# The conditioning projection of a decoder step: from one block ahead of everything to eight units, six of them between the steps of attention

## The chip, the cores and the metric

The kernel runs on one core of one Trainium2 chip. The metric is the time of one execution in device microseconds, from the first to the last instruction of the core. Three runs of the kernel before took 3728.18, 3729.02 and 3730.79 us.

## The reference, cut to what matters

One step of a two-layer decoder trunk for a prompt of 512 tokens and 8 sample sequences, D_MODEL 1024, all in float32. Each sub-layer is steered by a conditioning vector c: a linear map gives its shift, scale and gate. Layer 0 mixes tokens by latent attention, layer 1 by pooling; both are followed by a mixer that gathers 128 experts for each token.

```
def adaln(c, w, b):
    return jnp.split(jax.nn.silu(c) @ w + b, 6, axis=-1)      # w: (1024, 6144) for each of two layers

for l in range(DEPTH):
    sp = adaln(c_prompt, w_ada[l], b_ada[l])                  # 1 row
    ss = adaln(c_sample, w_ada[l], b_ada[l])                  # 8 rows
    hp = modulate(rmsnorm(xp, norm_mix[l]), sp[0], sp[1])     # then the mixer: attention or pooling
    xp = xp + sp[2][:, None, :] * mp
    hp = modulate(rmsnorm(xp, norm_ffn[l]), sp[3], sp[4])
    xp = xp + sp[5][:, None, :] * peer(hp, w_peer_q[l], peer_subkeys[l], peer_u[l], peer_v[l])
```

So the projection multiplies 9 rows by two matrices of 1024 x 6144: 50.3 MB of weights. Of its 2 x 6 parts of 1024 columns, the first three of layer 0 are wanted by the first normalization; the next two by the experts' first normalization, at the end of attention; the rest later.

## The kernel before

The program writes out each engine's instructions in order, and semaphores join them. Nothing reorders it: what stands first on an engine or on SP's DMA queue goes first. It has three stages.

**Projection.** 24 blocks of 512 columns (12 a layer). SP loads a block of 2 MB into one of four slots of the big buffer; TensorE multiplies it by `cact`, silu of c, 128 x 9 for each of 8 row chunks, into bank 0 or 1 (8 matmuls of 512 columns; in float32 the profile shows two instructions for each); VectorE adds the bias into a stage; SP stores the 9 x 512 result to `ada_rows` in DRAM. Behind block 18, SP reads the first parts of layer 0 back (`mods`, `sample_mods`). The attention weights are loaded behind the last blocks, since they lie in the same buffer.

**Attention of layer 0.** Five token tiles: the samples (8 rows) first, then four prompt tiles of 128. The steps on TensorE are `latents` (transposes of h, then 16 matmuls by w_in, in two halves), `project` (transposes of z, 9 matmuls by w_uq, 4 by w_uk), `turn_heads` (24 transposes), `sample_absorb`, and for each prompt tile `attend` and `mix_out`. ScalarE copies each result out of its bank, VectorE normalizes (`latents_norm`, `rows_norm`, `heads_norm`). The order up to the first `attend`: latents 0, latents 1, project 0, project 1, latents 2, turn_heads 1, project 2, sample_absorb, latents 3. This is the stretch that the change fills. `w_out`, the output projection's weights, is loaded into the ring behind it.

**Experts.** A loop of turns t from -25. From turn 0 on each turn handles two experts of every token of a tile: GpSimd gathers their rows of 1 MB each into 8 slots by indirect DMAs, VectorE forms dots, ScalarE the activation, TensorE accumulates (L1056). The work beside it is tied to turn numbers: queries and key scores of the eight heads (L908, L923), for which SP loads `wk`, one load a head, two buffers; and the cached pages of the sample sequences, which SP loads through a page table, and which TensorE first turns at turn 1. Before turn -25, SP has loaded `wk` of heads 0 and 1; then it waits for `x_mixed` (the last add of attention), loads the page table, four rows of modulation and 16 pages, and only then enters the turns, in which the load of head 2 stands first. TensorE multiplies by it from turn -2 on (`queries`), between the two matmul groups of L967 that spread the first tile's hidden rows for VectorE (L1829).

Of the kernel before, what the change touches and what calls it, by code (L numbers as in the profile page):

```python
# [50 lines left out]
ADA = 6 * D  # L51

# [30 lines left out]
def decoder_step(nc, T, O):  # L83

    ctx = ExitStack()
    with ctx:
# [49 lines left out]
        w_ada = big[:, :].rearrange("p (s c n) -> p s c n", s=4, c=DC)  # L136
# [22 lines left out]
        qs_s = ring[:, 0:2, :].rearrange("p a n -> p (a n)")[:, 0:NH * QH]  # L159
        ks_s = ring[:, 2, :]  # L160
# [16 lines left out]
        cact = hbuf[:, 2, 0:DC * NC].rearrange("p (c n) -> p c n", c=DC)  # L177

        ada_stage = work[0:NC, W - D:W].rearrange("p (b n) -> p b n", b=2)

        def ada_bias(l):
            return work[0:NC, 0:ADA] if l == 0 else ring[0:NC, 0:6, :].rearrange("p a n -> p (a n)")
# [92 lines left out]
        LAST_OUT = -14  # L275
        rows_of = lambda n: P if n < S0 else SROWS
# [86 lines left out]
        for name in ("first_in", "first_set", "own_used", "o_ready0", "o_ready1", "x_in", "consts_in", "c_in", "b_in", "table_in", "mix_w_in0", "mix_w_in1", "mix_w_in2", "mix_w_in3", "mix_w_in4", "out_w_in", "gains_in", "rot_in",  # L363
                     "mods_in", "pool_in", "state_in", "rows_out", "own_out", "own_in",
                     "y_out", "state_out", "dve_step", "act_step", "slot_turn", "gain_s_in", "pool_gain_in", "smp_mods_in", "link_done", "wait_done", "rank_step", "smp_step", "gate_in", "smp_gate_in", "wk_in0", "wk_in1", "pst_out", "mix_w_free", "smp_w_in0", "smp_w_in1"):
            sem(name)
# [4 lines left out]
        def _(sp):  # L371
# [7 lines left out]
            for l in range(DEPTH):  # L379
                ld(ada_bias(l),  # L380
                   T["b_ada"][l].partition_broadcast(NC), "b_in")
# [12 lines left out]
            def store_ada(i):  # L394
                l, j = divmod(i, ADA // 512)
                ld(ada_rows[l, :, j * 512:(j + 1) * 512], ada_stage[:, i % 2, :], f"ada_out{i % 2}")

            for l in range(DEPTH):
                for j in range(ADA // 512):
                    i = l * (ADA // 512) + j  # L400
                    if i >= 4:
                        sp.wait_ge(sem("ada_ps"), i - 3)
                    ld(w_ada[:, i % 4], T["w_ada"][l].rearrange("(c p) n -> p c n", p=P)[:, :, j * 512:(j + 1) * 512],
                       f"ada_w_in{i % 4}")
                    if i == 3:
                        for t in range(NT):
                            ld(x_tok[:, t, :], T["x_prompt"][0, t * P:(t + 1) * P, :], "x_in")
                        ld(x_tok[0:NS, NT, :], T["x_sample"].rearrange("b s d -> (b s) d"), "x_in")
                    if i >= 2:
                        sp.wait_ge(sem("ada_row"), i - 1)  # L410
                        store_ada(i - 2)
                    if i == ADA // 512 + 6:

                        for k in range(2):
                            sp.wait_ge(sem(f"ada_out{k}"), 16 * (ADA // 512 // 2))
                        mods(mod_mix, 0, 0, "prompt", P, T["norm_mix"][0])
                        sample_mods(0, 0)

            blocks = 2 * ADA // 512
            for n_, (dst, src, size) in enumerate(((w_in, T["w_mla_in"][0], DC * ZW), (w_uq, T["w_uq"][0], QLC * NH * QH),  # L420
                                                   (w_uk, T["w_uk"][0].rearrange("c h d -> c (h d)"), KLC * NH * NOPE),
# [1474 lines left out]
```

## Time and profile before

| | |
|---|---|
| Runs, median (lowest to highest) | 3729.02 us (3728.18 to 3730.79) |
| Profiled execution: time, span | 3729.29 us, 3727.5 us |
| TensorE busy | 2980.5 us (80%) |
| VectorE, ScalarE, GpSimd busy | 2313.5, 1049.1, 1221.7 us |
| Moved by DMA | 1266.81 MB, mean 340 GB/s |
| Chain that ended last | PE 45%, DMA 25%, DVE 15%, issue 7%, ACT 4% |

PE is TensorE, PEld its weight loads, DVE VectorE, ACT ScalarE, POOL GpSimd, SP the engine that issues most DMAs. A row of the timeline gives the start, how long the merged instructions lasted, engine, line, operation, tiles and count, and in brackets how long the engine had been idle and what ended that. The span has three parts: the projection until about 187 us, attention until about 628 us, and the expert turns, which fill the rest and move most of the bytes.

### The profile page before, as it was taken

How to read it: one execution, taken by the hardware profiler on the slowest of the kernel's cores; microseconds unless marked ns; L12 is line 12 of the kernel's file. 1: busy time of each engine (PE TensorE's matmuls, PEld its weight loads, DVE VectorE, ACT ScalarE, POOL GpSimd, SP SyncE). 2: the span in 40 equal slices, each digit the busy share in tenths (PEclk: the TensorE clock that was granted, in tenths of full speed). 3: DMA queues.
4: the chain of work that ended last, by engine and by line, in shares of the span. 5: the costliest groups of instructions: out<-in, count | busy, mean ns of one | idle time of the engine just before them, and what ended most of it. 6: DMA issues, size and time to landing. Idle time of an engine off the chain costs nothing.

```text
span 3727.5 us, 39795 instructions
## 1 busy us (share of the span) xinstructions
PE 2980.5 (80%) x11339; PEld 1299.6 (35%) x11339; DVE 2313.5 (62%) x6432; ACT 1049.1 (28%) x4465; POOL 1221.7 (33%) x1061
## 2 busy tenths in 40 slices
PE   8977886797888985898989868979876775586757
PEld 1235554443434432343444334434321231122311
DVE  0155444688778785677777576777866545555463
ACT  0012221343343441343444413434311111111111
POOL 0000000243333332443444434434444344434452
PEclk9987898898999997899999989999987777667775
DMA  9911002799999998999999999999999999979996
GB/s 316 333 52 60 33 1 109 300 402 360 415 359 383 413 402 323 403 413 400 411 413 392 418 360 416 404 404 412 392 409 405 422 415 410 347 266 413 421 420 168
DMA packets 217305, 1266.81 MB, mean 340 GB/s; under 512 B 22867, under 2 KB 43620, under 8 KB 77283
## 3 DMA queue, kind: packets, MB, share of 16 engines
q0 software_dynamic: 150016, 1090.59, 72.9%
q1 hardware_dynamic: 67069, 173.69, 12.6%
q8 instruction: 90, 1.47, 0.2%
q14 instruction: 130, 1.06, 0.1%
HBM read 1260.86 MB, written 3.79 MB: 339 GB/s over the span
## 4 chain that ended last, share of the span: by engine, by line
PE 45%; DMA 25%; DVE 15%; issue 7%; ACT 4%; POOL 2%; SPq 2%; DVEq 0%; POOLq 0%; ACTq 0%; PEldq 0%
PE bank L1056 16%; DMA ring<-in_uv,work 11%; PE bank L796 7%; DMA mod_mix<-in_uv,work 7%; DMA big<-in_uv,work 5%; PE bank L908 5%; PE bank L600 4%; DVE ring L1842 2%; PE bank L813 2%; PE bank L739 1%; PE bank L626 1%; ACT work L1330 1%; PE bank L651 1%; SPq L375 1%; POOL ring L1363 1%
## 5 line engine op out<-in xcount | busy, mean ns | idle before, releaser
L1056 PE MATMUL bank<-ring,work 128*64 128x512 f32 (+1 forms) x2112 | 945.2, 720 | 269.9 <-ACT work L1330 269.6
L1363 POOL DMA_INDIRECT ring<-in_uv,work x528 | 614.8, 1164 | 968.5 <-PE bank L1056 868.5
L1842 DVE CUSTOM_DVE_ANT_0 ring<-ring,mod_smp 128x1024 f32<-128x1024 f32 x512 | 621.9, 1224 | 261.9 <-DMA ring<-in_uv,work 253.1
L1363 POOL DMA_INDIRECT big<-in_uv,work x264 | 314.0, 1189 | 1088.5 <-DVE work L1733 623.8
L1317 ACT ACTIVATE work<-work 128x2 f32<-128x2 f32 (+1 forms) x528 | 107.3, 203 | 1542.6 <-DVE work L1842 1538.3
L796 PE MATMUL bank<-big 128*128 128x512 f32 x1024 | 516.6, 628 | 0.0
L1056 PE MATMUL bank<-big,work 128*64 128x512 f32 (+1 forms) x1056 | 332.6, 734 | 154.9 <-ACT work L1330 153.8
L1056 PEld LDWEIGHTS bank<-ring,work 128*64 128x64 f32 (+1 forms) x2112 | 215.4, 153 | 657.6 <-ACT work L1330 387.4
L1842 DVE CUSTOM_DVE_ANT_0 big<-big,mod_smp 128x1024 f32<-128x1024 f32 x256 | 309.8, 1224 | 141.6 <-DMA big<-in_uv,work 136.1
L1056 PE MATMUL bank<-work 128*64 128x512 f32 (+1 forms) x528 | 306.6, 709 | 105.3 <-ACT work L1330 104.8
L1330 ACT ACTIVATE work<-small,work 128x64 f32<-128x64 f32 (+1 forms) x1056 | 309.3, 340 | 192.9 <-DVE work L1853 136.4
L1182 ACT ACTIVATE bank<-bank 128x128 f32<-128x128 f32 x1024 | 270.1, 264 | 171.4 <-PE bank L796 155.0
L1056 PE MATMUL bank<-mod_mix,work 128*64 128x512 f32 (+1 forms) x528 | 317.7, 732 | 0.0
L908 PE MATMUL bank<-big 128*128 128x256 f32 x1024 | 237.3, 386 | 40.3 <-DMA big<-in_wk 39.0
L1363 POOL DMA_INDIRECT work<-in_uv,work x132 | 145.8, 1105 | 373.5 <-PE bank L1056 363.9
L796 PEld LDWEIGHTS bank<-big 128*128 128x128 f32 x1024 | 176.1, 192 | 215.4 <-issue 212.1
L908 PEld LDWEIGHTS bank<-big 128*128 128x128 f32 x1024 | 194.7, 193 | 89.1 <-DMA big<-in_wk 40.7
L1853 DVE TENSOR_TENSOR work<-work 128x2 f32<-128x2 f32 (+1 forms) x528 | 82.1, 155 | 219.3 <-ACT work L1317 210.2
L1842 DVE CUSTOM_DVE_ANT_0 mod_mix<-mod_mix,mod_smp 128x1024 f32<-128x1024 f32 x128 | 156.6, 1223 | 93.2 <-DMA mod_mix<-in_uv,work 93.2
L1056 PEld LDWEIGHTS bank<-big,work 128*64 128x64 f32 (+1 forms) x1056 | 76.3, 154 | 357.1 <-ACT work L1330 178.4
L1182 ACT ACTIVATION_READ_ACCUMULATOR bank<-bank 128x1 f32 x1024 | 193.6, 189 | 0.0
L1842 DVE CUSTOM_DVE_ANT_0 work<-work,mod_smp 128x1024 f32<-128x1024 f32 x128 | 156.6, 1224 | 43.5 <-DMA work<-in_uv,work 40.9
(277 smaller groups left out, 3634.0 us busy)
## 6 DMA issues: line engine op xcount, KB each, us to landing
big<-in_wk SPq DMA_DIRECT2D x48, 1152.0 KB
big<-in_w_ada SPq DMA_DIRECT2D x24, 2048.0 KB, 8.6
work<-in_cache_mla SPq DMA_DIRECT2D x104, 160.0 KB
ring<-in_uv,work POOLq DMA_INDIRECT x528
big<-in_uv,work POOLq DMA_INDIRECT x264
ring<-in_w_mla_out SPq DMA_DIRECT2D x1, 4096.0 KB, 13.3
big<-ada_rows SPq DMA_DIRECT2D x8, 512.0 KB, 7.4
big<-in_w_mla_out SPq DMA_DIRECT2D x4, 1024.0 KB, 13.1
```

The costliest lines, as they stand in the source:

```text
L375: sp.dma_start(dst, src).then_inc(sem(name), 16)
L600: last = mm(pb[i % 2][0:NC, :], cact[:, c, :], w_ada[:, i % 4, c, :], start=(c == 0), stop=(c == DC - 1))
L796: last = mm(pb[2 + half][:, :], cachedT[:, c * P:(c + 1) * P], w_uk[:, c, half * 512:(half + 1) * 512], start=(c == 0), stop=(c == KLC - 1))
L813: last = mm(pb[6][0:NH, 160:160 + KL], ps_s[:, g, :], cached[g][:, 0:KL] if g < NPG else cached_own, start=(g == 0), stop=(g == NPG))
L908: last = mm(pb[0][:, side * 2 * P:(side + 1) * 2 * P], wk[i % 2][:, c * 2 * NK + side * NK:c * 2 * NK + (side + 1) * NK], hT2[:, c, :], st ...
L1056: last = mm(out, diag[0:rows, t % 2, j, 0:min(m, HALF)], s[0:rows, D + half * 512:D + (half + 1) * 512], start=(k == 0 and (n < S0 or j == ...
L1182: last = act.activation(k, k, ACT.Square, accum_out=kss[:, at:at + 1])
L1317: act.activation(acts[0:m, t % 2 * GRP:(t % 2 + 1) * GRP], dots[0:m, t % 2 * GRP:(t % 2 + 1) * GRP], ACT.Gelu)\
L1330: act.activation(diag[0:m, t % 2, j, 0:o], scale_rows, ACT.Copy, scale=wts[0:m, at:at + 1]).then_inc(sem("diag_set"), 1)
L1363: pool.indirect_dma_start(slot[g % SLOTS][0:m, :], None, T["uv"].rearrange("l e d -> (l e) d"), bass.IndirectOffsetOnAxis(index[0:m, k * G ...
L1842: dve.tensor_tensor_reduce(u, u, hb[0:m, :], 1.0, 0.0, ALU.mult, ALU.add, dots[0:m, at:at + 1]).then_inc(sem("dots_set"), 1)
L1853: tt(wts[0:m, cols], acts[0:m, cols], g_all[0:m, k * GRP:(k + 1) * GRP], ALU.mult).then_inc(sem("wts_set"), 1)
```

## The change

The projection is cut into 8 units of 1536 columns (4 a layer). A unit has 9 slices: 8 of 128 rows of weights (128 x 1536, 786 KB) and one that is the bias row, multiplied by a row of ones. A slice is 4 matmuls of 384 columns; each writes another group of 32 partitions of one bank, so each uses another 32 columns of the array. `cact` is padded with zeros from 9 to 32 columns. Four slots in the ring hold slices. Units 0 and 1 come first; the 54 slices of the other six are put into the steps up to the first `attend` by `ADA_PLAN`, 0 to 4 at each of 19 points. ScalarE copies a finished unit out of its bank (in place of VectorE's bias adds), GpSimd stores it in four DMAs (in place of SP's stores). To free banks 6 and 7, early transposes go to banks 4 and 5, with waits for `z_ready`. Attention weights have their place from the start, so w_in and w_uq are loaded beside the units. SP's block that waits for `x_mixed`, with page table and pages, moves behind the loads of heads 2 and 3, to turn -5.

```
+UNIT = ADA // 4
+UGRP = UNIT // 4
+NSLICE = DC + 1
+ADA_SLOTS = 4
+        ada_bank = lambda u: pb[u if u < 2 else 7]
+        ADA_PLAN = (0, 2, 2, 2, 3, 3, 3, 3, 3, 3, 3, 3, 3, 3, 3, 3, 4, 4, 4)
# SP
+            def ada_slices(a, b):
+                for n in range(a, b):
+                    u, c = divmod(n, NSLICE)
+                    l, k = divmod(u, 4)
+                    if n >= ADA_SLOTS:
+                        sp.wait_ge(sem("ada_used"), n - ADA_SLOTS + 1)
+                    cols = slice(k * UNIT, (k + 1) * UNIT)
+                    if c < DC:
+                        ld(ada_slot[n % ADA_SLOTS], T["w_ada"][l, c * P:(c + 1) * P, cols], f"ada_w_in{n % ADA_SLOTS}")
+                    else:
+                        ld(ada_slot[n % ADA_SLOTS][0:1, :], T["b_ada"][l:l + 1, cols], f"ada_w_in{n % ADA_SLOTS}")
+            ada_slices(0, ADA_SLOTS)
+            ld(x_tok[0:NS, NT, :], T["x_sample"].rearrange("b s d -> (b s) d"), "x_in")
+            for t in range(NT):
+                ld(x_tok[:, t, :], T["x_prompt"][0, t * P:(t + 1) * P, :], "x_in")
+            ada_slices(ADA_SLOTS, NSLICE + 5)
+            load_mix_w(0)
+            ada_slices(NSLICE + 5, 2 * NSLICE)
+            load_mix_w(1)
+            ada_stored(2)
+            mods(mod_mix, 0, 0, "prompt", P, T["norm_mix"][0])
+            sample_mods(0, 0)
...
+            ada_slices(2 * NSLICE, 2 * NSLICE + ADA_SLOTS)
...
+            ada_slices(2 * NSLICE + ADA_SLOTS, UNITS * NSLICE)
             for i, t in enumerate(mla_order):
                 w.next("row_ready")
...
+                    sp.wait_ge(sem("ada_used"), UNITS * NSLICE)
+                    ada_stored(UNITS)
                     ld(w_out, T["w_mla_out"][0].rearrange("(c p) n -> p c n", p=P), "out_w_in")
...
+                if t == -5:
+                    sp.wait_ge(sem("x_mixed"), NT)
+                    ld(pages, T["page_table"].rearrange("(a s) g -> a (s g)", a=1), "table_in")
...
+                    load_pages(0)
# TensorE
+            def ada_slices(count):
+                for _ in range(count):
...
+                    pe.wait_ge(sem(f"ada_w_in{n % ADA_SLOTS}"), 16 * (n // ADA_SLOTS + 1))
+                    if c == 0 and u >= 3:
+                        pe.wait_ge(sem("ada_row"), u)
+                    k = slice(0, P) if c < DC else slice(0, 1)
+                    for g in range(4):
+                        last = mm(ada_bank(u)[g * UROWS:(g + 1) * UROWS, 0:UGRP], cact[:, c, :] if c < DC else ones[0:1, 0:UROWS],
+                                  ada_slot[n % ADA_SLOTS][k, g * UGRP:(g + 1) * UGRP], start=(c == 0), stop=(c == DC))
+                    last.then_inc(sem("ada_used"), 1)
# project(i) on TensorE
+                zq, zk = (pb[4], pb[5]) if i <= 2 else (pb[6], pb[7])
+                if i <= 2:
+                    pe.wait_ge(sem("z_ready"), (2, 2, 3)[i])
# ScalarE
+                act.activation(ada_stage[u % 2], ada_bank(u)[:, 0:UGRP], ACT.Copy).then_inc(sem("ada_row"), 1)
# GpSimd
+                for g in range(4):
+                    at = k * UNIT + g * UGRP
+                    pool.dma_start(ada_rows[l, :, at:at + UGRP], ada_stage[u % 2][g * UROWS:g * UROWS + NC, :]).then_inc(sem(f"ada_out{u % 2}"), 16)
```

On TensorE at the start of the program, before: L600 is the projection, L609 transposes of h, L626 the matmuls of `latents`, L640 to L643 the transposes of `project`, L651 and L654 its matmuls.

```order
L600 MATMUL bank<-big,hbuf 9x512 x192
L609 MATMUL bank<-small,hbuf 128x8 x8
L626 MATMUL bank<-big,hT 8x352 x16
L609 MATMUL bank<-small,hbuf 128x128 x8
L626 MATMUL bank<-big,hT 128x352 x16
L640 MATMUL bank<-small,hbuf 128x8 x3
```

The same place of the program now (line numbers have moved: L609 is the projection, L628 and L650 are transposes and matmuls of `latents`, L667 the first transposes of `project`):

```order
L609 MATMUL bank<-ring,work 32x384 x32
L609 MATMUL bank<-ring,ones 32x384 x4
L609 MATMUL bank<-ring,work 32x384 x32
L609 MATMUL bank<-ring,ones 32x384 x4
L628 MATMUL bank<-small,hbuf 128x8 x8
L650 MATMUL bank<-big,hT 8x352 x8
L609 MATMUL bank<-ring,work 32x384 x8
L650 MATMUL bank<-big,hT 8x352 x8
L628 MATMUL bank<-small,hbuf 128x128 x8
L609 MATMUL bank<-ring,work 32x384 x8
L650 MATMUL bank<-big,hT 128x352 x8
L609 MATMUL bank<-ring,work 32x384 x8
```

Of 192 matmuls of 512 columns, 72 of 384 columns are left in front; the others stand between the steps.

On SP's queue at the end of attention, before (`out_rows_p` are stores of latent rows, `in_wk` the heads' weights):

```order
L375 DMA big<-ada_rows 128x1024 x2
L375 DMA out_rows_p<-work 128x320 x2
L375 DMA big<-in_norm_ffn 128x1024
L375 DMA big<-in_wk 128x2304 x2
L375 DMA big<-in_page_table 1x128
L375 DMA work<-ada_rows 128x1024 x3
L375 DMA work<-in_norm_ffn 128x1024
```

The same place now:

```order
L380 DMA big<-ada_rows 128x1024 x2
L380 DMA out_rows_p<-work 128x320 x2
L380 DMA big<-in_norm_ffn 128x1024
L380 DMA big<-in_wk 128x2304 x4
L380 DMA big<-in_page_table 1x128
L380 DMA work<-ada_rows 128x1024 x3
L380 DMA work<-in_norm_ffn 128x1024
```

Two more loads of `in_wk` stand ahead of the page table; before, they stood behind the 16 page loads.

## Rows read from the trace of the kernel before

**Rows 1.** Chain that ended last, 0 to 700: start, us, what.
```profile
2.58 13.90 DMA big<-in_w_ada
16.62 118.67 PE bank L600 x272
...
186.59 1.24 DVE mod_mix L1399
```
**Rows 2.** Windows: length, busy us of each engine, TensorE clock, DMA share, GB/s.
```profile
40.00:60.00 20.00, 20.00 (x47) 4.18 (x46) 1.52 (x3) 0.00 (x0) 0.00 (x0) 1.00 1.05 384
50.00:100.00 50.00, 50.00 (x118) 10.63 (x117) 4.75 (x7) 0.00 (x0) 0.00 (x0) 1.00 0.92 321
```
**Rows 3.** DMA issues 0 to 620: KB each, median us to landing.
```profile
ring<-in_w_mla_out SPq DMA_DIRECT2D x1, 4096.0 KB, 13.3
```
**Rows 4.** Timeline of GpSimd and SP: issues of a gather, of a store.
```profile
626.18 0.94 POOL L1363 DMA_INDIRECT big<-in_uv,work  x1 [0.31 <-issue]
129.21 0.28 SPq L375 DMA_DIRECT2D ada_rows<-work  x1
```
**Rows 5.** Timeline of SP: rows read back, and the issue behind them.
```profile
136.47 1.31 SPq L375 DMA_DIRECT2D mod_mix<-ada_rows  x3
139.52 0.40 SPq L375 DMA_DIRECT2D big<-in_w_ada  x1
```
**Rows 6.** Timeline of TensorE, expert turns: two 64-column groups, and what follows.
```profile
700.32 0.64 PE L1056 MATMUL bank<-ring,work 128*64 128x512 f32 x1
700.33 0.64 PE L1056 MATMUL bank<-mod_mix,work 128*64 128x512 f32 x1
700.80 0.59 PE L1056 MATMUL bank<-ring,work 128*64 128x512 f32 x1
705.15 1.94 PE L1056 MATMUL bank<-big,work 128*64 128x512 f32 x8
707.02 1.98 PE L796 MATMUL bank<-big 128*128 128x512 f32 x4
```
**Rows 7.** Timeline of TensorE's weight loads there.
```profile
700.80 0.14 PEld L1056 LDWEIGHTS bank<-ring,work 128*64 128x64 f32 x1 [0.29 <-issue]
```
**Rows 8.** What TensorE waited for, 194 to 330: total, times, longest.
```profile
PE bank L626 <- ACT hT L1078: 6.8, 4, 3.7
PE bank L663 <- DVE hbuf L1483: 4.4, 1, 4.4
PE bank L640 <- issue: 3.9, 1, 3.9
PE bank L651 <- ACT work L1078: 3.8, 3, 1.4
PE bank L675 <- ACT hbuf L1078: 3.4, 1, 3.4
PE bank L640 <- ACT ring L1078: 3.3, 1, 3.3
```
**Rows 9.** Timeline of ScalarE: z copied out; TensorE: last step before `attend`, first of `mix_out`.
```profile
223.11 0.96 ACT L1078 ACTIVATE hbuf<-bank 128x352 f32<-128x352 f32 x2 [11.30 <-PE bank L626]
314.72 12.62 PE L626 MATMUL bank<-big,hT 128*128 128x352 f32 x32 [1.37 <-ACT hT L1078]
358.77 3.60 PE L739 MATMUL bank<-ring,hbuf 128*128 128x512 f32 x8
```
**Rows 10.** Timeline, end of attention: TensorE, VectorE, SP.
```profile
624.16 3.55 PE L967 MATMUL bank<-hbuf,small 128*64 128x512 f32 x8
666.72 6.38 PE L908 MATMUL bank<-big 128*128 128x256 f32 x16 [39.01 <-DMA big<-in_wk]
675.02 1.29 DVE L1829 TENSOR_SCALAR mod_smp<-bank 128x512 f32<-128x512 f32 x2 [39.67 <-PE bank L967]
634.69 20.05 SPq L375 DMA_DIRECT2D work<-in_cache_mla  x13
```
**Rows 11.** Windows there, columns as in rows 2.
```profile
625.00:670.00 45.00, 5.99 (x16) 3.11 (x13) 9.18 (x38) 2.37 (x3) 7.45 (x8) 0.54 0.92 354
670.00:685.00 15.00, 11.93 (x53) 7.36 (x51) 8.96 (x26) 3.05 (x8) 1.44 (x2) 0.93 0.04 9
```

More of the change, by code:

```diff
@@ L158, in decoder_step @@
         z_s = hbuf[:, 2, 0:ZW]
-        qs_s = ring[:, 0:2, :].rearrange("p a n -> p (a n)")[:, 0:NH * QH]
-        ks_s = ring[:, 2, :]
+        ring_all = ring[:, :, :].rearrange("p a n -> p (a n)")
+        ada_slot = [ring_all[:, j * UNIT:(j + 1) * UNIT] for j in range(ADA_SLOTS)]
+        qs_s = ring_all[:, ADA_SLOTS * UNIT:ADA_SLOTS * UNIT + NH * QH]
+        ks_s = hbuf[:, 2, :]
+        ada_stage = [pT[0][:, 0:UGRP], ring_all[:, ADA_SLOTS * UNIT + NH * QH:ADA_SLOTS * UNIT + NH * QH + UGRP]]
+        ada_bank = lambda u: pb[u if u < 2 else 7]
         rot_at = ZW + QH + NOPE + NH * QH
@@ new lines, in ada_stored, with load_mix_w @@
+            def ada_stored(units):
+                for k in range(2):
+                    sp.wait_ge(sem(f"ada_out{k}"), 16 * 4 * units // 2)
+            mix_w = ((w_in, T["w_mla_in"][0]), (w_uq, T["w_uq"][0]), (w_uk, T["w_uk"][0].rearrange("c h d -> c (h d)")),
+                     (w_uv, T["w_uv"][0].rearrange("c h d -> c (h d)")))
+            def load_mix_w(k):
+                ld(mix_w[k][0], mix_w[k][1].rearrange("(c p) n -> p c n", p=P), f"mix_w_in{k}")
+            ada_slices(0, ADA_SLOTS)
@@ L467, in _ @@
             sp.wait_ge(sem("first_set"), 1)
-            sp.wait_ge(sem("x_mixed"), NT)
-            ld(pages, T["page_table"].rearrange("(a s) g -> a (s g)", a=1), "table_in")
-            mods(mod_ffn, 0, 3, "prompt", P, T["norm_ffn"][0], gain)
-            sp.wait_ge(sem("rows_out"), 16 * (NT + 1))
-            sp.wait_ge(sem("own_out"), 16)
-            ld(s_own, own_dram.rearrange("(a s) h -> a (s h)", a=1), "own_in")
-            w.next("smp_clear")
-            w.next("table_in", 16)
             def load_pages(r):
@@ L594, in _, with ada_point @@
             w.next("c_act")
-            for i in range(2 * ADA // 512):
-                w.next(f"ada_w_in{i % 4}", 16)
-                if i >= 2:
-                    pe.wait_ge(sem("ada_row"), i - 1)
-                for c in range(DC):
-                    last = mm(pb[i % 2][0:NC, :], cact[:, c, :], w_ada[:, i % 4, c, :], start=(c == 0), stop=(c == DC - 1))
-                last.then_inc(sem("ada_ps"), 1)
+            w.next("ones_set")
+            ada_at = [0]
+            def ada_slices(count):
+                for _ in range(count):
+                    n = ada_at[0]
+                    ada_at[0] += 1
+                    u, c = divmod(n, NSLICE)
+                    pe.wait_ge(sem(f"ada_w_in{n % ADA_SLOTS}"), 16 * (n // ADA_SLOTS + 1))
[6 more added lines that the diff above has]
+                    last.then_inc(sem("ada_used"), 1)
+            ada_point_no = [0]
+            def ada_point():
+                if ada_point_no[0] < len(ADA_PLAN):
+                    ada_slices(ADA_PLAN[ada_point_no[0]])
+                ada_point_no[0] += 1
+            ada_slices(2 * NSLICE)
             def transpose_h(t, hb):
@@ L624, in latents @@
                 for half in range(2):
+                    if half:
+                        ada_point()
                     for c in range(DC):
@@ L762, in _ @@
                     latents(t + 4)
-            w.next("ones_set")
             def turn_page(r, g):
```

136 lines of the change are left out of this document (68 added, 68 removed).

## The prediction

> **What bounds the kernel now.** I read the chain that ended last first. Until 187 us it is the projection alone: a load until 16.6 us, then L600 on TensorE, and VectorE's first use of the modulation at 186.59 [rows 1]. The windows say why: TensorE is busy for the whole of each, at full clock, with 2.36 matmul instructions a microsecond, each 512 columns in 0.43 us [rows 2]. The DMA engines carry 321 to 384 GB/s beside it, so TensorE ends last, DMA close behind. Only 9 of the array's 128 columns are in use. Second, the waits of TensorE between 194 and 330 us: the six long ones sum to 25.6 us [rows 8], none of them for a DMA. The DMA queue has little to do there: the w_out load is nearly the only big one. Third, the timeline where attention ends: TensorE stands for 39.01 us before the queries of head 2, until `wk` lands, and VectorE 39.67 us behind it for L967; SP spends that time on pages [rows 10]. From 670 to 685 us the DMA engines carry 9 GB/s [rows 11].
>
> **Part 1, the projection in front.** It loses 6 of its 8 units. What is left is either bound by bytes or by columns.
> Bytes: slice 17 is landed behind 16 slices of 0.786 MB (12.6), the tokens (2.1) and w_in (2.9): 17.6 MB. At 384 GB/s [rows 2] that is 46 us; it starts at 2.58 us [rows 1] and lands some 2.8 us after its last byte (w_out, 4.19 MB in 13.3 us [rows 3], is 10.9 us of data and 2.4 more): 51 us. Before reads its weights in rows of 2 KB, the change in rows of 6 KB; I leave the rate.
> Columns: the nearest row is L1056, where two groups of 64 columns are in use. Both groups' instructions start together (700.32 and 700.33) and the next pair starts 0.48 us later; eight instructions and the switch to a full-array matmul take 1.87 us (705.15 to 707.02) [rows 6], where serial ones would take 3.4. Their weight loads of 0.14 us lie inside [rows 7]. So two groups overlap fully. Four groups of 384 columns, two instructions each, are 8 x 0.32 = 2.57 us in series and 0.64 us if four overlap as two do. The bounds are these two; I take 0.64, since the row that shows column groups shows them in parallel, and 0.15 us for a switch of groups (1.87 less 4 x 0.43). 18 slices are then 12 us, far under the loads' pace of 2.05 us a slice: DMA bound. In series they would be 46 us, still level with it.
> Behind slice 17: 1.3 us of TensorE, 0.5 us of ScalarE's copy, then GpSimd's four stores. The trace has no plain store from GpSimd; its gathers take 0.94 us and 0.30 us between them, SP's stores 0.28 us [rows 4]. I take the gathers' 1.25 us: 5.0 us, and 2.4 us to land. SP then issues the reads back, 3.05 us until the next issue [rows 5], of 2.2 MB (5.8 us) plus 2.4 us to land, say 8.5 us. Sum: 51 + 1.3 + 0.5 + 5.0 + 2.4 + 8.5 = 69 us, against 186.6: **118 us earlier**. Ends: stores at SP's 0.28 us and loads at 400 GB/s give 62; loads at 321 GB/s [rows 2] give 78: 108 to 125.
>
> On DMA the Trainium skill (DMA: Bandwidth & Descriptors, Specifications) gives about 358 GB/s as the HBM limit for a core; by it the 17.6 MB would take 49 us and the forecast be 3 us later. The trace disagrees: 384 here [rows 2].
>
> **Part 2, six units inside attention.** 54 slices at 0.64 us plus a switch for each of 18 bursts are 37 us of TensorE. I walked the steps in order, adding each burst, and took it out where TensorE waits anyway: bursts behind transposes (ScalarE copies 1.4 us meanwhile), behind project 0, 1 and 2 (3.3 to 3.7 us), and before turn_heads 1 and project 2 (4.4 and 3.9 us) [rows 8]. That hides about 19 of the 37; of the 25.6 us of waits not all lie where a burst stands. 18 us stay on the path, mostly the bursts between matmul groups.
> The refill: a burst of three needs one slice already there and two whose slots came free in the burst before. At 2.05 us of data and 2.4 to land they are there 6.5 to 7 us later. Steps of 8 to 10 us (w_uq's matmuls, a half of `latents`) cover that, and the 3.45 us of w_uk's is followed by a wait. Only the last bursts, of four slices with short steps between, come too close: in my walk 4 us of waiting before latents 3's matmuls, and 1 us in `sample_absorb`, where slice 63 needs bank 7, which ScalarE empties only after the q_abs copies.
> New wait for banks 4 and 5: project 0's transposes now wait until ScalarE has copied z, 0.96 us [rows 9], on the path: 1.2 us. Project 1's and 2's are long satisfied. In the queue: the gains are issued behind 3.1 MB of attention weights and four slices, 17 us of data; they are wanted some 23 us behind the modulation, so they fit, just. Behind 50 slices SP stands until TensorE has used slice 67; row stores and `own_scores` are late, and nobody waits for them until the pages. w_out is issued 7 us after slice 71 (copy, stores) and takes 13.3 us [rows 3]; latents 3's second half and `attend` lie between slice 71 and `mix_out`, and from 327 to 358.77 us `attend` alone is 31 us [rows 9]. Hidden. The bias adds that VectorE loses were off the path.
> Two to three microseconds more for slices that meet the clock at 1.2 GHz. **Together 26 us later**: 18 + 5 + 1.2 + 2. Ends: with the bursts wholly in the waits, and less of the stretch at half clock, 10; with nothing hidden (37) and twice the refill waits, 50.
>
> **Part 3, head 2 ahead of the pages.** Its load now waits only for head 0's scores and lands some 20 us before TensorE wants it. The L908 at 666.72 can follow the L967 that ends at 627.7, so TensorE and VectorE's L1829 could come 39 us earlier [rows 10]. What is late next is DMA: the first gathers, modulation and pages. Between 625 and 670 us 354 GB/s x 45 = 15.9 MB moved [rows 11]; heads 2 and 3 (1.18 MB each) leave that traffic for an idle stretch. 14.7 MB at 384 to 400 are 37 to 38 us, so DMA is through at 663 and goes on with the next gathers, which before began at 683-685; with head 3's 3 us that is 25. So 25 us if the turns that follow are DMA bound, 39 if they aren't. Page issues begin when they did (the table waits for `x_mixed`), 13 in 20.05 us [rows 10], and turn 1 needs only four. I take 30 us earlier. Lowest end 10 us, if turn 1 waits for its pages behind eight gathers.
>
> **Sum.** The profiled execution took 3729.29 us, 0.3 above the median of the runs: 3729 - 118 + 26 - 30 = **3607 us**. Everything behind hangs on turn order and keeps its length.
>
> **Rivals.**
> *The groups don't overlap* (2.57 us a slice). For it: four groups are nowhere in the trace. Against: two overlap fully. 54 slices are 139 us more less 25.6 of cover, 113; the front some 3 more; 3729 - 115 + 113 + 1 + 2 - 30 = 3700. 6%.
> *Weight loads stay exposed.* Four groups bring 8 weight loads a slice; at 0.14 us each [rows 7] outside the matmuls a slice is 1.8 us: 54 x 1.12 = 60 us more, 8 of it hidden: 3659. Against: L1056's lie inside. 5%. The Trainium skill has the rule behind this (TensorE: Matmul & The Clock Gate, Part 3): weight loads overlap running matmuls only if they address other row groups, and here all groups use all rows. By it this rival would be the forecast; rows 6 and 7 show the contrary for two groups that share all rows.
> *The ring of four is too small*: a slice lands 8 us after its slot is free, and each of 17 bursts waits 2 to 3 us: 3645. For it: only two or three loads are in flight. Against: the pace of [rows 2]. 8%.
> *The 39 us come back*: the first turns wait for pages or gathers, and part 3 gives 5: 3632. 8%.
> *Slower than before*: groups in series and at half clock, since the bursts keep being interrupted: 5.1 us a slice, 277 us in attention less 25 of cover, 92 instead of 49 us in front: 3729 - 118 + 43 + 252 + 3 - 30 = 3879. It decides from the slice cost at which 54 of them, less the cover, eat 118 + 30, about 3.2 us a slice. 2%.
>
> **How the numbers follow.** The forecast has 71%; its own range, 118 (-10, +7), 26 (-16, +24) and 30 (-20, +9), not all at their ends together, is 3583 to 3642. The range for 8 in 10 takes in the two near rivals and part of the weight loads': 3580 to 3652. 0.2% (7.5 us) is about what a measurement can tell from no change. Only the serial rival at half clock is slower; cases between it and no gain get 1% each way: faster 0.96, same 0.01, slower 0.03.
>
> **What would show it.** The first modulation product on VectorE near 69 us, not 187, with DMA at 380 GB/s before it and TensorE mostly waiting for slices. A slice's eight instructions in 0.64 to 0.7 us; 2.57 would mean series, 1.8 exposed loads. In the stretch from there to the first `attend`, 141 us before, some 166 now, with waits for slices of a few us in total and none for w_out. At the end of attention no wait for `wk`, and L1829 right behind the second L967. I am wrong if TensorE's waits for slices sum to over 15 us, if the reads back land after 80 us, or if the distance from the last `mix_out` to the first expert turn shrinks by less than 20 us.

## The result, and the profile after

The changed kernel takes 3600.55 us (median of 4 runs, 3592.32 to 3605.52) where the kernel before took 3728.6 us beside it: a ratio of 0.9652, with a 95% interval of 0.9636 to 0.9669. The forecast was 3607 us with a range of 3580 to 3652. The profiled execution is the fastest of the four, 3592.32 us with a span of 3590.5.

**The front.** The timeline of VectorE shows its first modulation product, which was at 186.59 [rows 1], and the chain that ended last shows the way to it (start, us, what):

```profile
68.76 1.23 DVE L1463 SCALAR_TENSOR_TENSOR mod_mix<-mod_mix,hT 128x1024 f32<-128x1024 f32 x1 [62.98 <-DMA hT<-in_norm_mix]
```
```profile
37.50 14.04 DMA ring<-in_w_ada
51.58 2.98 PE bank L609 x16
54.59 0.50 ACT ring L1124
55.13 0.53 issue
55.66 1.53 POOL ada_rows L1413 x3
57.19 1.69 DMA ada_rows<-ring
...
60.28 8.35 DMA hT<-in_norm_mix
```

The last slice of weights is used at 51.58, where the working had it landed at 51. Behind it come a slice and a bias slice on TensorE, ScalarE's copy of the bank, GpSimd's stores and the reads back. TensorE now waits for slices for 28.7 us of the front, which the groups by line say (0 to 68 us; busy us, mean ns of one, idle before):

```profile
L609 PE MATMUL bank<-ring,work 128*32 128x384 f32 x128 | 23.5, 825 | 28.7 <-DMA ring<-in_w_ada 28.7
```

and the windows (columns as in [rows 2]) show the DMA engines full instead of TensorE, which is busy for 25.78 of 48 us; its slices take 1.51 us each there, at half clock:

```profile
7.00:55.00 48.00, 25.78 (x144) 3.62 (x144) 0.00 (x0) 0.90 (x2) 2.22 (x4) 0.75 1.01 393
55.00:69.00 14.00, 0.00 (x0) 0.00 (x0) 0.24 (x1) 0.08 (x1) 2.04 (x4) 0.50 0.68 201
```

**Attention.** Latents 0 starts at 77.2 us and `attend(0)` at 230.8; before it was 194.9 and 327.2 (the window below begins at 194.8). That stretch has grown from 132.4 to 153.6 us. Here it is in one window, first of the kernel before, then of the changed one:

```profile
194.80:327.20 132.40, 105.00 (x329) 56.27 (x330) 68.36 (x185) 22.62 (x46) 0.00 (x0) 0.82 0.14 51
```
```profile
77.20:230.80 153.60, 137.66 (x761) 59.81 (x762) 68.20 (x184) 25.52 (x52) 12.29 (x24) 0.92 0.69 252
```

TensorE was idle for 27.4 us of it, and now for 15.9. Its groups by line there give the bursts 48.0 us (weight slices and bias slices):

```profile
L609 PE MATMUL bank<-ring,work 128*32 128x384 f32 x384 | 41.9, 530 | 7.9 <-DMA ring<-in_w_ada 7.1 <-ACT work L1124 0.8
L609 PE MATMUL bank<-ring,ones 1*32 1x384 f32 x48 | 6.1, 582 | 0.0
```

All other matmuls of the stretch, the same work as before, took 137.7 - 48.0 = 89.7 us instead of 105.0. The granted clock goes with it: 0.92 instead of 0.82. So the 21.2 us are 48.0 for bursts, less 15.3 us that the other matmuls took less at the higher clock, less 11.5 us of idle time. The timeline of TensorE shows slices at full clock (8 instructions in 0.85 us alone, 24 in 2.14, so 0.65 for each further slice and 0.71 on average) and a place where it goes wrong:

```profile
138.32 2.14 PE L609 MATMUL bank<-ring,work 128*32 128x384 f32 x24
140.39 3.70 PE L683 MATMUL bank<-big,work 128*128 128x512 f32 x8
...
147.49 0.85 PE L609 MATMUL bank<-ring,work 128*32 128x384 f32 x8
150.55 1.29 PE L609 MATMUL bank<-ring,work 128*32 128x384 f32 x8 [2.20 <-DMA ring<-in_w_ada]
151.77 1.50 PE L609 MATMUL bank<-ring,ones 1*32 1x384 f32 x8
153.20 7.19 PE L650 MATMUL bank<-big,hT 128*128 128x352 f32 x16
160.32 2.14 PE L609 MATMUL bank<-ring,work 128*32 128x384 f32 x24
162.39 5.00 PE L650 MATMUL bank<-big,hT 128*128 128x352 f32 x16
```

The wait of 2.20 us is for a slice of the ring, and behind it sixteen matmuls take 7.19 us, where the same number takes 5.00 a little later. A second such place is at 211.81: waits of 2.48, 0.94 and 0.43 us for slices, and 5.90 us for the sixteen matmuls. In a third TensorE is at work throughout: the 32 matmuls of 8 columns in `sample_absorb`, 196.7 to 202.0 us, have a granted clock of 0.68, and the two slices behind them take 2.79 us.

**The end of attention.** What stood in [rows 10] is answered by these of TensorE and VectorE: no wait for `wk`, and the pages' wait in its place.

```profile
535.53 3.72 PE L941 MATMUL bank<-big 128*128 128x256 f32 x16
...
537.55 1.28 DVE L1893 TENSOR_SCALAR mod_smp<-bank 128x512 f32<-128x512 f32 x2
...
563.82 0.69 PE L807 MATMUL bank<-small,work 128*128 128x128 f32 x2 [18.09 <-DMA work<-in_cache_mla]
```

Windows there, which answer to [rows 11]; no stretch at 9 GB/s is left:

```profile
527.50:572.50 45.00, 23.49 (x91) 12.43 (x89) 28.03 (x87) 10.36 (x29) 11.47 (x12) 0.71 0.99 374
572.50:587.50 15.00, 15.00 (x76) 6.76 (x72) 14.51 (x54) 7.28 (x40) 6.91 (x7) 1.00 0.98 402
```

The 25th gather on GpSimd is a good mark, since from there on both kernels do the same. Its row of before, and of after:

```profile
732.29 0.94 POOL L1363 DMA_INDIRECT big<-in_uv,work  x1 [2.45 <-PE bank L1056]
```
```profile
607.70 0.94 POOL L1433 DMA_INDIRECT big<-in_uv,work  x1 [2.47 <-PE bank L1089]
```

So up to this mark 124.6 us are gained: 117.8 in front (186.59 to 68.76), 21.4 given back from there to `attend(0)`, and 28.2 from `attend(0)` to the mark (405.1 us before, 376.9 now). From the mark to the end it is 2997.0 us before and 2992.9 by the median of the runs. In these two and the kernels below, which do the same there, the distance from the 25th to the 1045th gather lies between 2911 and 2924 us, so 4 us there mean nothing.

### The profile page after: what moved, and what is told of

It is laid out like the page before. It is cut to its first block, busy times and chain, and to the rows that moved or that the text cites. A ratio compares the mean times of both kernels' runs of the same rounds, so it can differ in the third digit from the quotient of the medians.

```text
span 3590.5 us, 40191 instructions
## 1 busy us (share of the span) xinstructions
PE 2848.8 (79%) x11531; PEld 1264.3 (35%) x11531; DVE 2295.5 (64%) x6409; ACT 1049.6 (29%) x4473; POOL 1224.3 (34%) x1093
## 3 DMA queue, kind: packets, MB, share of 16 engines
q8 instruction: 92, 1.51, 0.2%
## 4 chain that ended last, share of the span: by engine, by line
PE 42%; DMA 28%; DVE 15%; issue 7%; ACT 4%; POOL 2%; SPq 1%; DVEq 0%; POOLq 0%; ACTq 0%; PEldq 0%
PE bank L1089 17%; DMA ring<-in_uv,work 10%; DMA mod_mix<-in_uv,work 7%; DMA big<-in_uv,work 6%; PE bank L829 6%; PE bank L941 5%; DVE ring L1906 2%; DMA ring<-in_w_ada 2%; PE bank L846 2%; PE bank L650 2%; PE bank L774 2%; ACT work L1393 1%; DMA work<-in_cache_mla 1%; PE bank L609 1%; PE bank L679 1%
## 5 line engine op out<-in xcount | busy, mean ns | idle before, releaser
L1433 POOL DMA_INDIRECT ring<-in_uv,work x528 | 603.3, 1143 | 967.0 <-PE bank L1089 853.3
L829 PE MATMUL bank<-big 128*128 128x512 f32 x1024 | 509.4, 620 | 0.0
## 6 DMA issues: line engine op xcount, KB each, us to landing
ring<-in_uv,work POOLq DMA_INDIRECT x528, 11.5
big<-in_w_mla_out SPq DMA_DIRECT2D x4, 1024.0 KB, 11.5
```

Source lines behind the costliest of these rows:

```text
L829: last = mm(pb[2 + half][:, :], cachedT[:, c * P:(c + 1) * P], w_uk[:, c, half * 512:(half + 1) * 512], start=(c == 0), stop=(c == KLC - 1))
L1433: pool.indirect_dma_start(slot[g % SLOTS][0:m, :], None, T["uv"].rearrange("l e d -> (l e) d"), bass.IndirectOffsetOnAxis(index[0:m, k * G ...
```

## Experiments

All ratios are against the kernel before, timed on the same chip in the same session.

**1 and 2: part 3 undone, and part 3 alone.** In the changed kernel, the block with the page table, the FFN modulation and the pages goes back in front of the turns:

```diff
-                if t == -5:
+                if t == FIRST:
                     sp.wait_ge(sem("x_mixed"), NT)
```

> The changed kernel with SP's block (wait for x_mixed, page table, modulation, 16 pages) put back ahead of the loads of heads 2 and 3, nothing else undone. My theory: this part alone is worth the 27 us between the shift of the first gather (97.7 us earlier than before) and that of the gathers from the tenth on (about 125 us), so the time is 3628 us (3620 to 3636), with a wait of some 39 us for head 2's weights back in the trace. Rival: the order of the loads is worth nothing since DMA is saturated from there on anyway, and the 27 us come from the earlier start of something else: 3601 us.

Measured: 3621.49 us (3620.09 to 3627.27), ratio 0.9725 (0.9707 to 0.9743). Against 0.9652 that is 0.0073, or 27 us for part 3; the intervals of the two ratios make it 27 give or take 9. What TensorE waits for at the end of attention (500 to 600; total, times, longest) is again `wk`:

```profile
PE bank L941 <- DMA big<-in_wk: 38.3, 1, 38.3
```

In the kernel before, the same block moved behind the issue of `wk`, and nothing else:

```diff
             sp.wait_ge(sem("first_set"), 1)
-            sp.wait_ge(sem("x_mixed"), NT)
-            ld(pages, T["page_table"].rearrange("(a s) g -> a (s g)", a=1), "table_in")
...
-            load_pages(0)
...
+                if t == -5:
+                    sp.wait_ge(sem("x_mixed"), NT)
+                    ld(pages, T["page_table"].rearrange("(a s) g -> a (s g)", a=1), "table_in")
...
+                    load_pages(0)
```

> The kernel before with only that block moved to turn -5; the projection stays one block of 24 ahead of everything. Theory: the two parts of the change are independent and this one gives about 27 us: 3702 us (3693 to 3710). Rival: it pays only beside the new projection: 3729 us.

Measured: 3705.05 us (3703.72 to 3710.39), ratio 0.9947 (0.9928 to 0.9965), 20 us, give or take 7. TensorE's wait for `wk` is gone and this has come (600 to 700):

```profile
PE bank L775 <- DMA work<-in_cache_mla: 16.6, 1, 16.6
```

Its 25th gather is at 707.70, 24.6 us ahead of the kernel before. From `attend(0)` (329.27) to that gather it has 378.4 us against 405.1, which makes 26.7 us for part 3 beside the old projection; beside the new one it is 399.5 - 376.9 = 22.6 us, between experiment 1 and the changed kernel. These readings are sharper than the times, and the time of experiment 1 also has in it a stretch before `attend(0)` that is 6.9 us shorter (experiment 9). All of them lie at 20 to 27 us, not at the 39 of the wait that went. Of the 28.2 us gained between `attend(0)` and the mark, 5.6 stay when the block is put back (405.1 against 399.5); what gives them was not traced.

**3: is it the pages, or the bytes?** GpSimd holds its fifth gather, and with it those behind, until the first pages are in, so that pages and modulation don't share the DMA engines with them:

```diff
+                    if g == 4:
+                        pool.wait_ge(sem("page_in0"), 16 * PGRP)
+                        pool.sem_inc(sem("slot_turn"), 1)
```

> The changed kernel, but GpSimd issues the fifth to eighth gather only once the first four cached pages have landed. In the changed kernel TensorE stands 18.1 us at turn 1 for these pages, which share the DMA engines with eight gathers of 1 MB, while the DMA engines are busy throughout (share 1.0, 375 to 421 GB/s). Theory: the stretch is bound by bytes and the bytes are the same, so the wait shrinks to under 8 us and the time stays within 4 us of 3600. Rival: the wait is on the path, and the time falls by 8 to 15 us. Third: holding the gathers opens a hole in the DMA and costs up to 8 us.

Measured: 3598.36 us (3595.43 to 3605.64), ratio 0.9661 (0.9644 to 0.9677): no change. Yet the wait for pages (520 to 600) shrank from 18.1 us to this:

```profile
PE bank L807 <- DMA work<-in_cache_mla: 2.4, 1, 2.4
```

and the DMA engines are as full in the same windows as in the changed kernel:

```profile
527.50:572.50 45.00, 28.23 (x112) 13.74 (x110) 30.11 (x95) 12.06 (x39) 14.19 (x14) 0.83 0.98 377
572.50:587.50 15.00, 13.08 (x58) 5.70 (x55) 12.29 (x43) 5.17 (x31) 7.55 (x5) 1.00 1.01 421
```

The 25th gather came at 606.0 instead of 607.7. The order of the transfers decides who waits: VectorE now waits 15.8 us for gathers between 527 and 608 us, where it was 0.3. That fits a stretch bound by bytes, since the DMA engines have a share of 0.95 or more in both kernels up to that gather. It does not exclude TensorE: in the changed kernel it works without a gap from the pages' landing (563.82) to the 25th gather, which waits for it, and here from 582.92. So the wait for pages lies on the path. Shown is that it can't be traded for a wait for gathers at a profit, and not that it costs nothing.

**4: what the front's other loads cost.** The queue's order: 18 slices, then the tokens, the reads back, w_in, four slices, the gains, and only then the other attention weights.

```diff
-            ada_slices(0, ADA_SLOTS)
+            ada_slices(0, 2 * NSLICE)
...
-            ada_slices(ADA_SLOTS, NSLICE + 5)
-            load_mix_w(0)
-            ada_slices(NSLICE + 5, 2 * NSLICE)
-            load_mix_w(1)
...
-            load_mix_w(2)
-            load_mix_w(3)
-            ld(w_ukT, T["w_ukT"], "mix_w_in4")
+            load_mix_w(0)
...
+            for k in range(1, 4):
+                load_mix_w(k)
+            ld(w_ukT, T["w_ukT"], "mix_w_in4")
```

> The changed kernel with another order of loads in front: the 18 slices of units 0 and 1 first, then the tokens, then the modulation read back, then w_in and four slices, and the other attention weights behind the gains. Theory: the front is bound by bytes until slice 17 lands (17.6 MB, now 12.6 MB), so VectorE's first modulation product comes 12 us earlier than at 68.8 us and the time falls by 11 us, to 3589 (3583 to 3596). Rival: TensorE at 1.2 GHz (1.51 us a slice) or the ring of four slots sets the pace once no other loads stand between the slices, and less than 5 us are left: 3596 to 3601.

Measured: 3588.45 us (3584.24 to 3591.66), ratio 0.9629 (0.9613 to 0.9645). The first product is at 56.85, 11.9 us earlier, but `attend(0)` only 4.9 us (225.9), and the 25th gather 5.8 us (601.9). The median agrees with the expected 3589 us, but the trace shows only half of the 11 us behind it, and the interval overlaps that of the changed kernel; the hit is no proof of the theory. Here is what took most of the 7 us, in TensorE's timeline: slice 22 is late, and the matmuls behind the wait run at the lower clock.

```profile
92.91 1.51 PE L606 MATMUL bank<-ring,work 128*32 128x384 f32 x8 [5.10 <-DMA ring<-in_w_ada]
94.80 1.51 PE L606 MATMUL bank<-ring,work 128*32 128x384 f32 x8 [0.38 <-DMA ring<-in_w_ada]
96.24 7.29 PE L647 MATMUL bank<-big,hT 128*128 128x352 f32 x16
```

**5: without column groups.** Each chunk's four matmuls write the same 32 columns, summed, so that none can run beside another (ScalarE's copy and GpSimd's stores take these 32 partitions). The kernel leaves out three quarters of the modulation's columns.

```diff
-    last = mm(ada_bank(u)[g * UROWS:(g + 1) * UROWS, 0:UGRP], cact[:, c, :] if c < DC else ones[0:1, 0:UROWS],
-              ada_slot[n % ADA_SLOTS][k, g * UGRP:(g + 1) * UGRP], start=(c == 0), stop=(c == DC))
+    last = mm(ada_bank(u)[0:UROWS, 0:UGRP], cact[:, c, :] if c < DC else ones[0:1, 0:UROWS],
+              ada_slot[n % ADA_SLOTS][k, g * UGRP:(g + 1) * UGRP], start=(c == 0 and g == 0), stop=(c == DC and g == 3))
...
```

> The changed kernel, but the four matmuls of each chunk of a slice write the same 32 columns of the array (partitions 0 to 31 of the bank), one after the other, so no two of them can run side by side; ScalarE copies and GpSimd stores the same amount from there. It leaves out three quarters of the modulation's columns: each unit's four groups are summed into one. If column groups are what makes a slice cost 0.64 to 0.71 us, as the forecast has it, a slice is now 8 instructions of 384 columns in series, 2.57 us or a little more, 54 slices in attention cost some 103 us more, of which up to 6 lie in waits that are left, and the time is near 3697 us (3685 to 3715), with attend 0 some 97 us later than in the changed kernel. If the groups bring nothing and a slice is cheap for another reason (384 columns wide, 32 columns of weights), the time stays near 3600 us (3592 to 3612).

Measured: 3701.23 us (3700.17 to 3704.6), ratio 0.9924 (0.9908 to 0.994). 24 instructions, three slices, take 7.90 to 7.93 us in TensorE's timeline, against 2.14 above:

```profile
146.68 7.90 PE L609 MATMUL bank<-ring,work 128*32 128x384 f32 x24
154.41 3.60 PE L683 MATMUL bank<-big,work 128*8 128x512 f32 x8
```

That is 2.63 us a slice, close to the 2.57 of the forecast's rival of groups in series, which had 3700 us. The groups are worth 101 us: the stretch from latents 0 to `attend(0)` has 248.4 us, 94.8 more than in the changed kernel, and starts 8.9 us later. How four can overlap though every one needs its own weights shows in the weight loads of the changed kernel, then of this one (timeline of PEld):

```profile
144.02 0.16 PEld L609 LDWEIGHTS bank<-ring,work 128*32 128x32 f32 x8 [0.76 <-issue]
144.37 0.13 PEld L609 LDWEIGHTS bank<-ring,work 128*32 128x32 f32 x4 [0.19 <-issue]
```
```profile
147.00 0.11 PEld L609 LDWEIGHTS bank<-ring,work 128*32 128x32 f32 x1 [0.21 <-issue]
147.32 0.11 PEld L609 LDWEIGHTS bank<-ring,work 128*32 128x32 f32 x1 [0.21 <-issue]
```

With groups, four to eight loads lie within 0.13 to 0.16 us; without, one at a time, every 0.32 us. In neither kernel do they stand outside the matmuls: the series has 16 instructions in 5.35 us and 24 in 7.93, 0.32 for each.

**6: no bursts in attention.** All 72 slices in front, `ADA_PLAN = ()`.

> The changed kernel, but all 72 slices run in front of latents 0 and none inside attention; the column groups, the reads back of layer 0 after 36 slices, and the place of the pages' block stay. 64 weight slices of 0.786 MB, the tokens and w_in are 55.3 MB: at 390 GB/s TensorE is through with slice 71 near 148 us and latents 0 starts there, 71 us later than now (77). Against it stand the 21 us that bursts add to the stretch from the modulation to attend 0. Theory (bursts cost 21 us and hide DMA time of 71): 3600 + 71 - 21 = 3650 us (3642 to 3660). Rival (the bursts cost attention more than that stretch shows, up to the 47 us of their columns and waits): 3625 us or less. Rival (loads of attention's weights behind the slices then hold project 0): 3660 us or more.

Measured: 3672.65 us (3670.03 to 3686.74), ratio 0.9857 (0.9834 to 0.9879). The theory's time was missed by 23 us, and the wrong part was the front: latents 0 starts at 169.5 us, not 148. The second rival has the time (3660 or more) but not the cause: behind latents 0 TensorE waits for no load of weights. The expectation had left out the reads back and w_uq (4.6 MB, 12 us), and the rate fell:

```profile
55.00:148.00 93.00, 57.67 (x340) 8.23 (x344) 13.22 (x32) 2.46 (x5) 10.24 (x20) 0.60 0.96 364
```

From latents 0 to `attend(0)`, where the experiment speaks, it has 134.5 us without bursts, 19.1 less than the changed kernel and 2.1 more than before:

```profile
169.50:304.00 134.50, 106.98 (x332) 56.41 (x329) 62.84 (x169) 23.10 (x47) 2.05 (x4) 0.82 0.16 62
```

3600.5 + 92.3 - 19.1 = 3674, so the account closes. The row is also the control for the clock: new banks, waits and queue, but no bursts, and TensorE is at 0.82 and 107 us busy as in the kernel before. It is the bursts that bring 0.92. The other kernels agree: this stretch has 0.81 in experiment 2, without bursts, and 0.89 to 0.95 in each of those with them.

**7 and 8: other plans.** Experiment 7 is 4 with the plan (0,2,2,0,3,4,3,3,4,2,2,4,4,3,4,3,4,3,4); experiment 8 is the changed kernel with another plan alone.

```diff
-        ADA_PLAN = (0, 2, 2, 2, 3, 3, 3, 3, 3, 3, 3, 3, 3, 3, 3, 3, 4, 4, 4)
+        ADA_PLAN = (0, 2, 2, 2, 3, 4, 3, 3, 4, 2, 2, 3, 4, 3, 4, 3, 4, 2, 4)
```

> The changed kernel with the queue order of the experiment on the front (18 slices first, then the tokens, the reads back, w_in, four slices, the gains, the other attention weights, the remaining slices) and the plan (0,2,2,0,3,4,3,3,4,2,2,4,4,3,4,3,4,3,4): bursts are sized to the slices that can have landed by then. That order alone measured 3588 us with 10.5 us of waits for slices inside attention. If those waits are what gave back 7 of the 12 us that its front gained, they fall to 3 us or less and the time is 3582 us (3577 to 3587). If the time was given back by something else (the clock, the weights of project 0, the DMA behind), it stays at 3588 us (3585 to 3592).

> The changed kernel with its own queue order and another plan, (0,2,2,2,3,4,3,3,4,2,2,3,4,3,4,3,4,2,4): the same 54 slices, moved among the 19 places toward those behind which TensorE waits anyway. The changed kernel shows 7.1 us of waits for slices, and 2.2 us more of matmuls at the lower clock behind one of them. If these are what the place of the bursts decides, the time is 3594 us (3589 to 3598), with 3 us or less of waits for slices. If the total of slices that must be loaded between 58 and 215 us decides (260 GB/s of 400, so not bound), or the waits only move, it stays within 3 us of 3600.

Measured for 7: 3588.97 us (3581.56 to 3590.86), ratio 0.9614 (0.9599 to 0.9628), which is 3585 us beside a kernel before of 3728.6. The waits for slices did not fall (10.7 us against 10.5), but none is over 1.5 us, no group of matmuls behind one is slow, and `attend(0)` comes at 218.5, 7.4 us ahead of experiment 4. What TensorE waited for (55 to 330) in 7, then in 4 (55 to 230):

```profile
PE bank L606 <- DMA ring<-in_w_ada: 10.7, 12, 1.5
```
```profile
PE bank L606 <- DMA ring<-in_w_ada: 10.5, 7, 5.1
```

The time is the rival's (3588), not the theory's 3582. It is the fastest kernel measured: its interval is clear of the changed kernel's first one (0.9636 to 0.9669) and just touches the second (0.9626 to 0.9654, experiment 9). From experiment 4 it can't be told apart. Its theory named the wrong quantity, the sum of the waits, while the clock behind them is what moved: TensorE is busy for 135.9 us of the stretch instead of 141.4, at 0.94 instead of 0.89; 2.1 us more came from latents 0, which starts earlier. For 8: 3602.16 us (3599.55 to 3611.83), ratio 0.9667 (0.965 to 0.9685), no gain in the median. Its waits for slices total 7.2 us, as before, so the rival held: they moved. Its profile does reach `attend(0)` at 226.5 and the 25th gather at 603.2, 4.3 and 4.5 us earlier than the changed kernel's: gains of this size are lost in the 13 us by which the rest varies.

**9 and 10: once more, and a ring of three.** `ADA_SLOTS = 3` for the second.

> The changed kernel once more, in other executions, to see how much of the differences between the profiles of its attention stretch is the kernel's and how much the run's. Its first profile has 153.6 us from the start of latents 0 to attend 0, 7.1 us of them waits for slices, the longest 2.5 us, and matmuls of latents at the lower clock behind a wait of 2.2 us; the kernel that differs only far behind that stretch (pages' block early) had 146.7 us, 4.9 us of waits, the longest 1.2 us, and no such slow matmuls. Theory: the waits for slices vary from run to run and the clock follows the longer ones, so this stretch comes out anywhere between 146 and 155 us, with slow matmuls only behind a wait of about 2 us or more. Rival: the stretch is a fixed property of the kernel, and comes out at 153.6 within 1 us. Time 3600 us (3593 to 3607) in both.

> The changed kernel with three slots for slices in the ring instead of four. A burst of three then needs all three slots full, which takes some 2.4 us after the last matmul of the burst before plus 2.05 us for each slice still to come, up to 8.6 us, and each burst of four waits a further 4.5 us for its fourth slice. Theory (the ring's depth is what keeps the waits for slices at 7 us): they grow by 20 to 40 us, and the time is 3625 us (3612 to 3645). Rival (bytes per time decide, 260 GB/s of 400 over the stretch, and depth does not matter): waits of 12 us or less and 3605 us or less.

Measured for 9: 3598.84 us (3590.08 to 3601.31), ratio 0.964 (0.9626 to 0.9654). The stretch from latents 0 to `attend(0)` has 153.4 us, with the same two waits and the same slow matmuls:

```profile
150.26 1.47 PE L609 MATMUL bank<-ring,work 128*32 128x384 f32 x8 [2.33 <-DMA ring<-in_w_ada]
151.66 1.50 PE L609 MATMUL bank<-ring,ones 1*32 1x384 f32 x8
153.10 7.01 PE L650 MATMUL bank<-big,hT 128*128 128x352 f32 x16
```

The rival held: the stretch repeats within 0.2 us. Experiment 3 is a third profile of the same instructions up to there, taken on the chip and in the session of experiment 1, and has 153.5 us, with 7.29 us for the matmuls behind a wait of 2.21. Why experiment 1 had 146.7 us stays open: its slice landed about 1 us earlier and its clock stayed up. The chip and the session are excluded; whether it is the kernel or that one execution, a single profile can't say.

For 10: 3611.15 us (3605.72 to 3617.83), ratio 0.9672 (0.9658 to 0.9687), 12 us over experiment 9. The waits for slices doubled, the stretch took 165.0 us, 11.6 more, and it began 3.5 us later, since the front has the same ring:

```profile
PE bank L609 <- DMA ring<-in_w_ada: 14.5, 16, 2.3
```

Neither side had the size: the ring's depth matters, but the waits grew by 7 us where the theory asked for 20 to 40, and the time by half of the 25 it asked for. This kernel also shows that the length of a wait alone doesn't set the clock: behind its longest, the sixteen matmuls are not slow, while behind waits of 0.34 and 0.52 us (182.49, 184.38) the eighteen of w_uq take 10.80 us instead of 7.99.

```profile
159.26 0.85 PE L609 MATMUL bank<-ring,work 128*32 128x384 f32 x8 [2.30 <-DMA ring<-in_w_ada]
160.04 0.85 PE L609 MATMUL bank<-ring,ones 1*32 1x384 f32 x8
160.82 5.00 PE L650 MATMUL bank<-big,hT 128*128 128x352 f32 x16
```

## Why the prediction was right

**Part 1, 118 us: 117.8 measured**, with errors that cancel. The two stages taken from [rows 4] were off most: GpSimd's stores and their landing took 3.3 us (55.66 to 58.96) where 5.0 and 2.4 were said, since a plain store takes GpSimd 0.51 us and not a gather's 1.25. Against these 4.1 us stand 0.6 for the last landing, 1.7 because TensorE stood at half clock and was through with the last slice and the bias in 3.0 us instead of 1.3, 0.5 before the first store, and 1.3 in the reads back (9.8 us, not 8.5). For the landing of a last byte the working has 2.8 us in one place and 2.4 in the others, from one row, which gives 2.4 (13.3 less 10.9). That a slice costs nothing in a front bound by bytes held at half clock too. The DMA rate was 393 GB/s where 384 was taken [rows 2]; as to the Trainium skill's limit of 358 GB/s for a core (DMA: Bandwidth & Descriptors, Specifications), the trace disagrees in this window as well.

**Part 2, 26 us later: 21.4 measured.** The sum came near for reasons that are only half its own; that two misses cancel is luck. The cover was read well: of 27.4 us of idle time 8.0 are left when the 7.9 us of waits for slices and their banks are set aside, so 19.4 are filled where 19 were said. The refill waits were 7.9 us with the wait for bank 7, against 5. But the bursts took 48.0 us and not 37: 0.89 us for each slice, since a burst that is broken by a wait pays 0.85 for a slice alone, and some run at half clock (1.51). And the term for the clock had the wrong sign. The forecast had 2 us to pay; measured are 15.3 us gained on the other matmuls, over a stretch in which TensorE, fed in its waits, was granted 0.92 of its clock in place of 0.82. Experiment 6 shows that this comes with the bursts and goes with them. In the forecast it stood only at the low end ("less of the stretch at half clock"). The terms as measured are 48.0 - 19.4 + 7.9 - 15.3 = 21.2.

The column groups, on which all of it rests, are shown by experiment 5. The rule of the Trainium skill (TensorE: Matmul & The Clock Gate, Part 3), that weight loads overlap running matmuls only if they address other row groups, isn't what these rows show: all four groups use all 128 rows, and with their loads inside a slice costs 0.65 to 0.71 us.

**Part 3, 30 us earlier: 22.6 measured by the traces beside the new projection, 26.7 beside the old.** The working's DMA-bound value was 25 and its free value 39, and the forecast went between; the measured values lie by the first. In the sum its place was filled by 28.2 us, of which 5.6 are not its own: that the whole agrees so well is partly luck. TensorE's wait for pages, the low end's mechanism, did come: the first expert product on VectorE is 39.9 us closer to the last `mix_out`, and 18.1 us of that go to this wait. That the bytes set the end, whoever waits, fits the full DMA engines and experiment 3 but is not shown: TensorE, at work without a gap behind the wait, may set it as well.

Of the rivals, *groups don't overlap* has its time confirmed by the kernel that makes it true (3701 against 3700), *the ring of four is too small* (3645) is excluded by 7.1 us of waits for slices, and three slots cost only 12 us more, and *the 39 us come back* is excluded by experiments 1 and 2. *Weight loads stay exposed*, 1.8 us a slice, is excluded by 0.71. *Slower than before*, 5.1 us a slice in series at half clock, did not come even where the groups are in series: 2.63 us and a clock of 0.94 in experiment 5.

None of the signs of being wrong came: the waits for slices in the stretch were 7.1 us, the reads back were in by 68.6, and from the last `mix_out` to VectorE's first expert product it is 39.0 us where it was 79.0. This last sign says little, since it comes before the wait for pages: at the 25th gather 28.2 us are left. One sign of being right failed: TensorE was not mostly waiting for slices in front, since at half clock they kept it busy for 25.8 of 48 us.

Open is, besides the bound of part 3, what exactly tips the clock. A short wait is not needed for it: in experiment 5, TensorE has had no wait since 128.87 us when the granted clock is 0.62 between 174.5 and 179.0, and eighteen matmuls take 9.69 us there instead of 7.99. Taking a wait for slices away altogether wasn't tried; it needs a larger ring than the buffers leave.

## What to carry to other kernels

Work with few output columns cost about a quarter here (2.14 us against 7.90 for three slices) once it was spread over four groups of 32 columns, and then fits into another stage's waits; count it against the waits that are really idle where it stands. When TensorE is below full clock in a stretch, filling its gaps can pay twice: here the matmuls already there went from 105.0 to 89.7 us, so price them at the higher clock, too. When a wait goes, ask how many bytes the stretch behind it must move and what waits for them next: here the wait of 39 us went, one of 18 us came in its place, and 22.6 to 28.2 us were gained.

## What the runs showed of the hardware

- Four groups of 32 columns, f32, run side by side in full: 24 instructions of 384 columns in 2.14 us, and in 7.90 to 7.93 us when they share a group. Their weight loads, of 32 columns each, go eight in 0.16 us.
- A plain store issued by GpSimd takes 0.51 us of it, about half an indirect one (0.94).
- The stretch up to `attend(0)` took 153.6, 153.4 and 153.5 us in three profiles with the same instructions up to there, on at least two chips. A fourth had 146.7 us, with 4.9 instead of 7.1 us of waits for slices and a clock of 0.95 instead of 0.92.
- With the 54 slices between the steps the granted clock of this stretch was 0.89 to 0.95, without them 0.81 and 0.82. It also fell where TensorE had no wait: to 0.62 between 174.5 and 179.0 us in experiment 5.
- With GpSimd's gathers in flight (527 to 580 us), thirteen loads of 160 KB on SP's queue took a median of 13.1 us to land and one of 512 KB 19.2 us. Holding the gathers back for them moved waits and no time.
